# A token's second expert unit reads its partial row, and sums, norms and stores the finished row

## The chip, the cores and the metric

The kernel runs on one core of a Trainium2 chip, as one program. The metric is the device time of one execution in microseconds (us); less is better. The five engines are TensorE (PE), VectorE (DVE), ScalarE (ACT), GpSimd (POOL) and SyncE (SP); each takes its own instructions in order, and they wait for each other through semaphores. DMAs are issued from the queues of SyncE, ScalarE and GpSimd and run on 16 DMA engines.

## What is computed

Two transformer blocks over 512 tokens of width 1024, in float32. The first has sparse and sliding-window attention and a dense MLP; the second has gated linear attention, pooling, and a mixture of experts with a final norm. The change touches only the last of these:

```python
g_p, g_idx = lax.top_k(softmax(ht @ w_rg + b_rg), 1)         # one of 4 groups for each token
e_top, e_idx = lax.top_k(logits_of_that_group, 2)            # two of its 8 experts
gate = g_p * softmax(e_top)
y = (silu(h @ w_gate[e]) * (h @ w_up[e])) @ w_down[e]        # each expert, on its tokens
x = x + sum_of_two(gate * y)
out = x * rsqrt(mean(x * x) + eps) * norm_f_g                # the final norm
```

There are 32 experts (width 256); 512 tokens with two experts each make 1024 rows.

## The kernel before

The first 1040 us compute everything up to the router. The rest is the expert stage and the end. Rows are put into columns of 64: one column for each expert, and one extra column (number 16) for the rows of an expert that has more than 64. Two columns make a unit of 128 rows (unit 8 holds the extra column alone, with 64 rows twice over), so there are 17 units, 0 to 16 (`UNITS_E`, `LAST_E`). Columns of units 0 to 7 hold experts 0 to 15; the later ones hold the late experts, whose numbers are computed. If the expert that overflows is a late one, the extra unit takes it whole, and one column (`SPARE`, 18) has no expert.

For each unit, GpSimd gathers the tokens' rows from `x_rows` in DRAM into one of five buffers `xe` (L682); TensorE transposes them (L1945), and VectorE scales the result into `xeT` (L1687). TensorE multiplies by the gate and up weights `gu` (L2287); ScalarE applies Silu (L1106), VectorE the product (L1694), TensorE transposes, ScalarE copies to `hidT` (L1109), and TensorE multiplies by the down weights `dn` (L2304). VectorE multiplies by the gate and adds into `xe` (L1702, function `y_of`), which signals `y_made`. As each row of x was stored halved, the two rows of a token together hold x once. GpSimd scatters the unit's rows to `y2_rows` in DRAM (L686): the first choice of token t goes to row t, the second to row 512 + t.

SyncE loads the weights; a buffer is loaded again as soon as its unit is done (six buffers of a column for gate and up, eight for down). The spare column is loaded by GpSimd with indirect DMAs (L696), which skip rows whose number is out of bounds.

GpSimd's order in the loop over q = 0 to 15 is written out: at q = 7 the three loads of the spare column; then wait for `y_made` of unit q, scatter it, wait that the scatter of unit q-1 has landed, gather the rows of unit q+4. VectorE's order is: hidden product of unit q, transposed rows of unit q+2, `y_of(q)`.

At the end (L645 to L653) SyncE waits for the scatters of units 0 to 15 and reads both planes of `y2_rows` back, one block of 128 tokens after another. The last unit's rows are not scattered: TensorE puts them into place by a product with a one-hot matrix (`hot`, L2413) and for two blocks adds the planes too (L2419). VectorE sums (L1868, L1875), ScalarE squares (L1135 to L1144), VectorE refines the root (L1164 to L1167) and multiplies (L1877, L1884), SyncE stores `out` (L651).

The lists that all this goes by are made on VectorE between 1040 and 1092 us: `tabi` (rows and slots of each column), `slotv` (their factors), from the rank counts `pos`, `late_columns`, `place_overflow`, `list_overflow` and `name_late_experts`.

Of the kernel before, what the change touches and what calls it, by code (L numbers as in the profile page):

```python
# [5 lines left out]
F32 = mybir.dt.float32  # L6
# [7 lines left out]
P = 128  # L14
# [27 lines left out]
def late_at(n):  # L42


    c = (n - 2 * EXTRA_AT + 1) // 2
    return c - 1 if n % 2 else PAIRS - 1 if n == SPARE else c + PAIRS // 2 - 2


def places_of(q):

    return (2 * q, 2 * q + 1) if q < EXTRA_AT else (2 * q,) if q == EXTRA_AT else (2 * q - 1, 2 * q)
# [26 lines left out]
def expert_at(n):  # L78

    return n if n < 2 * EXTRA_AT else None  # L80
# [155 lines left out]
def gated_blocks(nc, A, out):  # L236
# [8 lines left out]
    with stack:  # L245
# [35 lines left out]
        def const(name, rows=P):  # L281
# [37 lines left out]
                 for n, at in mix_at.items()}  # L319
# [45 lines left out]
        tabi, over_n, steps64, over_at, spare_rows, tab_end = lay(low_at + words([P, 2, NK, P]) + words([P, 2, DE]),  # L365
                                       ("tabi", [P, 2, COLS], I32), ("over_n", [1, 2 * OVER + 1], I32), ("steps64", [P, 8]),
                                       ("over_at", [P, 2], I32), ("spare_rows", [P, 1], I32))
# [7 lines left out]
        y2 = place("y2", [P, NT, 2, D], top + 2 * half_buf)  # L375
        x_out = place("x_out", [P, 2, NT, P], base + 4 * CONST_COLS["cos"][0])
        zeros = place("zeros", [P, D], s_at + 2 * half_buf)
        hot = place("hot", [P, NT, P], base + 4 * CONST_COLS["before"][0])
# [9 lines left out]
        y2_rows = nc.dram_tensor("y2_rows", [2 * L, D], F32).ap()  # L388
# [33 lines left out]
        def for_overflow(e, over, block_of):  # L422
            with e.If(over > 1):
                with e.Fori(1, OVER) as i:
                    block_of(i)
                e.wait_ge(S("over_scattered"), 16 * (OVER - 1))
# [13 lines left out]
        def _(sp):  # L440
# [59 lines left out]
            for q in range(QUARTERS):  # L500
# [16 lines left out]
                for n in range(2 * q, 2 * q + 2):  # L517
                    sp.dma_start(y2_rows[n * P:(n + 1) * P, :], zeros[:, :]).then_inc(S("y_zeroed"), 16)
# [137 lines left out]
        def _(pool):  # L656
# [19 lines left out]
            row_bound, slot_bound = pool.to_reg(L - 1), pool.to_reg(2 * L - 1)  # L676
# [8 lines left out]
            def scatter(n, slots, done):  # L685
                pool.indirect_dma_start(y2_rows, bass.IndirectOffsetOnAxis(ap=slots, axis=0), xe[:, n, :], None,  # L686
                                        bounds_check=slot_bound, oob_is_err=False).then_inc(done, 16)
# [16 lines left out]
            pool.wait_ge(S("y_zeroed"), 16 * 2 * NT)  # L704
# [14 lines left out]
            def overflow(i):  # L719
# [5 lines left out]
                gather((LAST_E - 1) % X_BUFS, over_at[:, 1:2], S("over_gathered"))  # L725
# [4 lines left out]
                scatter((LAST_E - 1) % X_BUFS, over_at[:, 0:1], S("over_scattered"))  # L730

            pool.wait_ge(S("scattered1"), 16 * LAST_E // 2)
            for_overflow(pool, over, overflow)
            for n in range(X_BUFS):
# [14 lines left out]

# [1710 lines left out]
```

## Time and profile before

| what | us |
|---|---|
| median of 3 runs | 1302.31 |
| lowest, highest | 1302.14, 1302.82 |
| the profiled execution | 1302.32 |
| its span, first to last instruction | 1300.0 |
| TensorE busy in the span | 1267.6 (98%) |
| VectorE, ScalarE, GpSimd busy | 613.1, 460.4, 535.5 |
| mean granted TensorE clock | 0.994 of full |

The span is what the trace covers; a little lies around it. Busy time of TensorE counts matmuls in flight, so 98% is not TensorE at its peak. What a change to one stage does has to be read from that stage: its share of DMA, its waits, and the chain that ends last in it.

### The profile page before, as it was taken

How to read it: one execution, taken by the hardware profiler on the slowest of the kernel's cores; microseconds unless marked ns; L12 is line 12 of the kernel's file. 1: busy time of each engine (PE TensorE's matmuls, PEld its weight loads, DVE VectorE, ACT ScalarE, POOL GpSimd, SP SyncE). 2: the span in 40 equal slices, each digit the busy share in tenths (PEclk: the TensorE clock that was granted, in tenths of full speed). 3: DMA queues.
4: the chain of work that ended last, by engine and by line, in shares of the span. 5: the costliest groups of instructions: out<-in, count | busy, mean ns of one | idle time of the engine just before them, and what ended most of it. 6: DMA issues, size and time to landing. Idle time of an engine off the chain costs nothing.

```text
span 1300.0 us, 18634 instructions
## 1 busy us (share of the span) xinstructions
PE 1267.6 (98%) x6670; PEld 968.7 (75%) x6670; DVE 613.1 (47%) x1162; ACT 460.4 (35%) x770; POOL 535.5 (41%) x685
## 2 busy tenths in 40 slices
PE   8999999999999999999999999999999999999986
PEld 6767777787888888888888788777888875555552
DVE  4868768725542422222225765757243265222225
ACT  5657534435434324133144534145322210000102
POOL 4633323334555655555545664424644211121100
PEclk9999999999999999999999999999999999999999
DMA  7422222112334433434333333312426989999995
GB/s 221 107 65 56 66 58 66 50 49 81 98 96 113 131 97 97 130 98 129 97 98 114 97 93 85 83 49 67 128 81 268 362 323 394 424 421 424 424 423 240
DMA packets 212157, 211.38 MB, mean 163 GB/s; under 512 B 31903, under 2 KB 193425, under 8 KB 200817
## 3 DMA queue, kind: packets, MB, share of 16 engines
q1 hardware_dynamic: 203104, 200.25, 45.8%
q0 software_dynamic: 5184, 8.29, 1.7%
q10 hardware_dynamic: 3796, 1.86, 0.5%
q8 instruction: 46, 0.75, 0.2%
q14 instruction: 27, 0.22, 0.0%
HBM read 205.76 MB, written 16.78 MB: 171 GB/s over the span
## 4 chain that ended last, share of the span: by engine, by line
issue 39%; POOL 31%; PE 26%; DMA 1%; DVE 1%; POOLq 0%; ACT 0%; SPq 0%; DVEq 0%; ACTq 0%
POOL wlo L661 31%; PE bank L2287 8%; PE bank L2304 4%; PE bank L1915 3%; PE bank L1917 3%; PE bank L1916 3%; PE side L1945 2%; DMA y<-y_rows 1%; PE bank L1956 1%; DMA y_rows<-xe,tabi 1%; PE side L1917 1%; PE side L1915 1%; PE side L1916 1%; PE side L2203 1%; PE bank L2419 0%
## 5 line engine op out<-in xcount | busy, mean ns | idle before, releaser
L661 POOL TENSOR_TENSOR wlo<-raw,whi 128x256 fp32r<-128x256 f32 x644 | 498.2, 805 | 524.4 <-ACT whi L785 524.2
L1916 PE MATMUL bank<-actB_lo,whi 128*128 128x512 f32 x608 | 236.7, 389 | 0.0
L1915 PE MATMUL bank<-actB_hi,whi 128*128 128x512 f32 x576 | 227.7, 395 | 0.5 <-POOL wlo L661 0.5
L1917 PE MATMUL bank<-actB_hi,wlo 128*128 128x512 f32 x576 | 224.4, 390 | 0.0
L785 ACT ACTIVATE whi<-raw 128x1024 fp32r<-128x1024 f32 x161 | 169.0, 1051 | 151.8 <-PE bank L1917 124.9
L1915 PE MATMUL bank<-actA_hi,whi 128*128 128x512 f32 x400 | 157.3, 393 | 0.6 <-DVE actA_lo L1201 0.6
L1916 PE MATMUL bank<-actA_lo,whi 128*128 128x512 f32 x400 | 156.1, 390 | 0.0
L1917 PE MATMUL bank<-actA_hi,wlo 128*128 128x512 f32 x400 | 156.1, 390 | 0.0
L2287 PE MATMUL bank<-gu,xeT 128*64 128x256 f32 x1088 | 127.7, 384 | 4.7 <-issue 2.2
L1916 PEld LDWEIGHTS bank<-actB_lo,whi 128*128 128x128 f32 x608 | 114.2, 188 | 24.1 <-issue 1.0
L1915 PEld LDWEIGHTS bank<-actB_hi,whi 128*128 128x128 f32 x576 | 108.1, 188 | 25.9 <-issue 2.3
L1917 PEld LDWEIGHTS bank<-actB_hi,wlo 128*128 128x128 f32 x576 | 108.1, 188 | 22.8
L2287 PEld LDWEIGHTS bank<-gu,xeT 128*64 128x64 f32 x1088 | 80.7, 138 | 46.9 <-issue 15.2
L1938 PE MATMUL bank<-actA_hi,whi 128*128 128x512 f32 x216 | 95.0, 440 | 0.0
L1915 PEld LDWEIGHTS bank<-actA_hi,whi 128*128 128x128 f32 x400 | 75.5, 189 | 17.6 <-DVE actA_lo L1201 1.8
L1916 PEld LDWEIGHTS bank<-actA_lo,whi 128*128 128x128 f32 x400 | 75.5, 189 | 15.8 <-issue 0.2
L1917 PEld LDWEIGHTS bank<-actA_hi,wlo 128*128 128x128 f32 x400 | 75.4, 188 | 15.7
L686 POOL DMA_INDIRECT y_rows<-xe,tabi x16 | 16.3, 1018 | 168.4 <-DVE xe L1702 168.4
L1940 PE MATMUL bank<-actA_hi,wlo 128*128 128x512 f32 x216 | 85.0, 394 | 0.0
L1939 PE MATMUL bank<-actA_lo,whi 128*128 128x512 f32 x216 | 84.4, 391 | 0.0
L1396 DVE TENSOR_SCALAR relu_u<-bank 128x512 f32<-128x512 f32 x32 | 22.1, 692 | 128.7 <-PE bank L1917 128.7
L1106 ACT ACTIVATE hid<-bank,slotv 128x256 f32<-128x256 f32 x17 | 12.6, 740 | 167.8 <-PE bank L2287 167.8
(433 smaller groups left out, 1653.0 us busy)
## 6 DMA issues: line engine op xcount, KB each, us to landing
dn<-in_w_exp_down SPq DMA_DIRECT2D x32, 1024.0 KB, 16.0
raw<-in_w_in SPq DMA_DIRECT2D x57, 512.0 KB, 3.8
gu<-in_w_exp_gate SPq DMA_DIRECT2D x28, 1024.0 KB
gu<-in_w_exp_up SPq DMA_DIRECT2D x28, 1024.0 KB
raw<-in_w_up SPq DMA_DIRECT2D x32, 512.0 KB, 3.9
raw<-in_w_down SPq DMA_DIRECT2D x32, 512.0 KB, 3.6
raw<-in_w_out SPq DMA_DIRECT2D x16, 512.0 KB, 3.7
raw<-in_w_in SPq DMA_DIRECT2D x16, 256.0 KB, 3.1
```

Source lines behind the costliest of these rows:

```text
L661: ins = nc.gpsimd.tensor_tensor(wlo[:, slot, at], raw[:, slot, at], whi[:, slot, at].bitcast(F32), ALU.subtract)
L785: a(whi[:, c % RING, :], raw[:, c % RING, :], ACT.Copy).then_inc(hi_made, 1)
L1396: chain(v.tensor_scalar(relu_u[:, m % 2, :], out_bank(up + m)[:, :], 0.0, None, ALU.max), chunk_freed)
L1915: mm(b[:, :], w_hi, hi[:, k, :], start=first, stop=False)
L1916: mm(b[:, :], w_hi, lo[:, k, :], start=False, stop=False)
L1917: ins = mm(b[:, :], w_lo, hi[:, k, :], start=False, stop=last)
L1938: mm(b[:, :], w_hi, actA_hi[:, k, :], start=k == 0, stop=False)
L1939: mm(b[:, :], w_hi, actA_lo[:, k, :], start=False, stop=False)
L1940: ins = mm(b[:, :], w_lo, actA_hi[:, k, :], start=False, stop=k == NK - 1)
L1945: return nc.tensor.transpose(dst, src, ident[0:src.shape[0], 0:src.shape[0]])
L2287: ins = mm(b[ROWS * h:ROWS * (h + 1), g * DE:(g + 1) * DE], xeT[:, j, k, ROWS * h:ROWS * (h + 1)], gu[n % GU_BUFS][:, g, k, :], start=k == ...
L2304: ins = mm(bank[2 + n][ROWS * h:ROWS * (h + 1), :], hidT[:, j, k * P + ROWS * h:k * P + ROWS * (h + 1)], w[:, k, n * L:(n + 1) * L], start ...
```

## The change

No plane of y is read back at the end. The stored x is no longer halved. Each row has a turn: the earlier of a token's two units scatters x + its part to `part_rows` (512 rows instead of 1024); the later unit does not gather its x into the sum, but gathers the partial row over its `xe` row after TensorE has transposed it, adds its own part, and so has the finished row, which is squared (ScalarE, `squares_of`), normed (VectorE, `finish`) and stored straight to `out` by an indirect DMA (`store_rows`). Rows that a list leaves out carry a number out of bounds and are skipped. This holds for units 2 to 16. So that a token's two experts are never in neighbouring units, experts are renumbered: column n of the first 16 holds expert 8 (n mod 4) + n // 4.

GpSimd's order for each unit becomes: store of unit q-1, scatter of unit q, wait for that scatter's landing, gather of the partial rows of unit q+1, wait for the store's landing, gather of the x rows of unit q+4. VectorE gets `finish(q-1)`, which waits for the scatter of q-1, ahead of `y_of(q)`, and `y_of(q)` waits for its partial rows. ScalarE gets two table loads for each unit. At the end TensorE's one-hot products and sums, VectorE's sums and SyncE's reads and stores are gone; unit 16 goes the same way as the others.

The diff, cut to what matters (the overflow loop, which takes no part here, is left out):

```diff
 def expert_at(n):
-    return n if n < 2 * EXTRA_AT else None
+    return EPG * (n % NG) + n // NG if n < 2 * EXTRA_AT else None
+OVER_X = (LAST_E + 1) % X_BUFS
+FINISH_FROM = 2
...
         @block.sync
-            for j in range(2):
-                sp.wait_ge(S(f"scattered{j}"), 16 * LAST_E // 2)
-            for i in range(NT):
-                sp.dma_start(y2[:, i, :, :], y2_rows.rearrange("(k t p) n -> t p k n", k=2, p=P)[i])\
-                  .then_inc(S(f"block_in{i}"), 16)
-            for i in range(NT):
-                sp.wait_ge(S("final_out"), i + 1)
-                sp.dma_start(out[i * P:(i + 1) * P, :], y2[:, i, 1, :]).then_inc(S("stored"), 16)
-            sp.wait_ge(S("stored"), 16 * NT)
+            sp.wait_ge(S("rows_stored"), 16 * (UNITS_E - FINISH_FROM))
...
         @block.gpsimd
+            def gather_parts(n, tokens, done):
+                pool.indirect_dma_start(xe[:, n, :], None, part_rows, bass.IndirectOffsetOnAxis(ap=tokens, axis=0),
+                                        bounds_check=row_bound, oob_is_err=False).then_inc(done, 16)
+
+            def store_rows(n, tokens, done):
+                pool.indirect_dma_start(out, bass.IndirectOffsetOnAxis(ap=tokens, axis=0), xe[:, n, :], None,
+                                        bounds_check=row_bound, oob_is_err=False).then_inc(done, 16)
+
+            def scattered(q):
+                pool.wait_ge(S(f"scattered{q % 2}"), 16 * (q // 2 + 1))
+
+            def parts_of_unit(q):
+                pool.wait_ge(S("xe_used"), 2 * (q + 1))
+                gather_parts(q % X_BUFS, tabi[:, 2, q:q + 1], S("parts_in"))
+
+            def store_unit(q):
+                pool.wait_ge(S("rows_finished"), q - FINISH_FROM + 1)
+                store_rows(q % X_BUFS, tabi[:, 2, q:q + 1], S("rows_stored"))
...
             for q in range(LAST_E):
                 if q == EXTRA_AT - 1:
+                    pool.wait_ge(S("slots_ready"), 2)
                     spare_expert()
+                if q > FINISH_FROM:
+                    store_unit(q - 1)
                 pool.wait_ge(S("y_made"), q + 1)
                 scatter(q % X_BUFS, tabi[:, 0, q:q + 1], S(f"scattered{q % 2}"))
+                if FINISH_FROM <= q + 1 < LAST_E:
+                    scattered(q)
+                    parts_of_unit(q + 1)
                 n = q - 1 + X_BUFS
                 if n < UNITS_E:
                     if q == 0:
                         pool.wait_ge(S("over_listed"), 1)
                     else:
-                        pool.wait_ge(S(f"scattered{(q - 1) % 2}"), 16 * ((q - 1) // 2 + 1))
+                        scattered(q - 1)
+                    if q > FINISH_FROM:
+                        pool.wait_ge(S("rows_stored"), 16 * (q - FINISH_FROM))
                     gather(n % X_BUFS, tabi[:, 1, n:n + 1], S(f"gathered{n % X_BUFS}"))
...
+            parts_of_unit(LAST_E)
+            store_unit(LAST_E - 1)
+            store_unit(LAST_E)
+            pool.wait_ge(S("rows_stored"), 16 * (UNITS_E - FINISH_FROM))
...
         @block.scalar
+            def squares_of(q):
+                one_ = slice(q % NT, q % NT + 1)
+                nc.scalar.preload_act_table_set("natural_log_exp_and_others")
+                for n in range(2):
+                    act.wait_ge(*((S("y_made"), q + 1) if q < LAST_E else (S("last_y_made"), n + 1)))
+                    chain(a(side[3][:, :], xe[:, q % X_BUFS, n * L:(n + 1) * L], ACT.Square, accum_out=gw[:, 10 + n, one_]))
+                    if n == 0:
+                        chain(a(gw[:, 3, one_], gw[:, 10, one_], ACT.Identity, scale=1.0 / D, bias=eps_t[:, :]))
+                chain(a(gw[:, 14, one_], gw[:, 11, one_], ACT.Ln, scale=1.0 / D, bias=gw[:, 3, one_]))
+                chain(a(gw[:, 13, one_], gw[:, 14, one_], ACT.Exp, scale=-0.5), S("guess_made"))
             for q in range(LAST_E):
...
+                if q >= FINISH_FROM:
+                    squares_of(q)
+                    if q < LAST_E - 1:
+                        nc.scalar.preload_act_table_set("silu_and_others")
...
         @block.vector
             def y_of(q):
                 dve.wait_ge(S("down_done"), q + 1)
+                if q >= FINISH_FROM:
+                    dve.wait_ge(S("parts_in"), 16 * (q - FINISH_FROM + 1))
...
+            def finish(q):
+                one_ = slice(q % NT, q % NT + 1)
+                dve.wait_ge(S("guess_made"), guesses[0] + 1)
+                chain(v.tensor_tensor(gw[:, 12, one_], gw[:, 10, one_], gw[:, 11, one_], ALU.add))
+                refine(gw[:, 12, one_], gw[:, 13, one_], D, gw[:, 14, one_], gw[:, 15, one_])
+                if q < LAST_E:
+                    dve.wait_ge(S(f"scattered{q % 2}"), 16 * (q // 2 + 1))
+                chain(v.scalar_tensor_tensor(xe[:, q % X_BUFS, :], xe[:, q % X_BUFS, :], gw[:, 13, one_], gfin[:, :],
+                                             ALU.mult, ALU.mult), S("rows_finished"))
...
+                if q == 1:
+                    list_overflow()
                 if q + 2 < UNITS_E:
                     rows_turned(q % 2, q + 3)
-                if q == 1:
-                    list_overflow()
+                if q > FINISH_FROM:
+                    finish(q - 1)
                 y_of(q)
```

The lists get some more small VectorE steps: whose turn it is (`vals[:, :, 0]`), the tokens to finish (`tokens_to_finish`), the renumbering in `late_columns` and `name_late_experts`.

## Rows read from the trace of the kernel before

**Rows 1.** Windows: length, busy of PE, PEld, DVE, ACT, POOL, clock, DMA share, GB/s.

```profile
1112.00:1124.00 12.00, 12.00 (x92) 6.66 (x90) 3.12 (x6) 1.13 (x2) 2.03 (x2) 1.00 1.01 422
1252.00:1269.50 17.50, 14.55 (x100) 7.88 (x96) 2.08 (x4) 1.41 (x3) 1.84 (x2) 0.90 0.98 411
1269.50:1275.00 5.50, 4.08 (x34) 2.39 (x35) 0.66 (x1) 0.98 (x3) 0.00 (x0) 1.00 0.37 148
```

**Rows 2.** Chain that ended last, 1225 to 1300 us: start, duration, what.

```profile
1250.18 1.42 DVE xe L1702 x2
...
1251.87 0.99 POOL y_rows L686
...
1267.41 7.44 DMA y_rows<-xe,tabi
...
1275.89 10.13 DMA y<-y_rows
...
1296.20 0.75 DVE y L1884
```

**Rows 3.** VectorE timeline, 1053 to 1270 us: start, duration, what, idle before.

```profile
1079.47 0.69 DVE L1694 SCALAR_TENSOR_TENSOR hid<-bank,slotv,hid 128x256 f32<-128x256 f32 x1
...
1086.52 1.41 DVE L1702 SCALAR_TENSOR_TENSOR xe<-bank,slotv,xe 128x512 f32<-128x512 f32 x2 [3.32 <-PE bank L2304]
...
1098.54 1.41 DVE L1702 SCALAR_TENSOR_TENSOR xe<-bank,slotv,xe 128x512 f32<-128x512 f32 x2 [4.26 <-PE bank L2304]
...
1265.72 1.41 DVE L1702 SCALAR_TENSOR_TENSOR xe<-bank,slotv,xe 128x512 f32<-128x512 f32 x2 [6.56 <-PE bank L2304]
```

**Rows 4.** Page: span, software DMA queue (packets, MB, share of engines).

```profile
span 1300.0 us, 18634 instructions
...
q0 software_dynamic: 5184, 8.29, 1.7%
```

**Rows 5.** Line 686, scatter of a unit: ns, and us to landing.

```profile
DMA to landing us min/median/max: 7.4/8.1/9.7
```

**Rows 6.** Timeline of all engines, 1048 to 1058 us.

```profile
1049.64 1.20 POOL L682 DMA_INDIRECT xe<-x_rows,tabi  x1 [3.39 <-DVE tabi L1639]
...
1050.09 1.28 ACT L1094 ACT_TABLE_LOAD   x1
...
1051.04 0.17 DVE L1656 COPY vals<-con 128x8 f32<-128x8 f32 x1
...
1054.93 0.95 PEld L1945 LDWEIGHTS side<-con,xe 128*128 128x128 f32 x8 [0.31 <-DMA xe<-x_rows,tabi]
```

**Rows 7.** Line 682, gather of a unit, 1040 to 1060 us.

```profile
L682 POOL DMA_INDIRECT xe<-x_rows,tabi x4: 992/996/1196, 1049.6 to 1053.7; - x4
...
DMA to landing us min/median/max: 4.4/4.4/4.4
```

**Rows 8.** Line 682, 1080 to 1300 us.

```profile
DMA to landing us min/median/max: 10.0/10.0/10.1
```

**Rows 9.** DMAs issued 1112 to 1113.5 us (unit 3): count, landing.

```profile
y_rows<-xe,tabi POOLq DMA_INDIRECT x1, 8.5
```

**Rows 10.** Timeline of all engines, 1255 to 1300 us.

```profile
1269.46 3.67 PE L2287 MATMUL bank<-gu,xeT 128*64 128x256 f32 x32 [0.33 <-DMA gu<-in_w_exp_up]
...
1278.71 0.75 DVE L1854 SCALAR_TENSOR_TENSOR xe<-bank,slotv,xe 128x512 f32<-128x512 f32 x1 [0.97 <-PE bank L2404]
...
1291.85 0.60 ACT L1139 ACTIVATE xe<-bank 128x512 f32<-128x512 f32 x1
...
1292.91 1.28 DVE L1877 SCALAR_TENSOR_TENSOR y<-y,gw,gfin 128x1024 f32<-128x1024 f32 x1
...
1294.01 0.29 ACT L1143 ACTIVATE gw<-gw 128x1 f32<-128x1 f32 x1
```

**Rows 11.** DMA issues, 1040 to 1300 us.

```profile
out<-y SPq DMA_DIRECT2D x4, 512.0 KB, 2.6
...
gu<-in_w_exp_gate,spare_rows POOLq DMA_INDIRECT x1
```

More of the change, by code:

```diff
@@ L516, in _ @@
                 load_group(C_MLP + 2 * NK * q + NK, NK, w_down_v[:, NK * q:NK * (q + 1), :], 0)
-                for n in range(2 * q, 2 * q + 2):
-                    sp.dma_start(y2_rows[n * P:(n + 1) * P, :], zeros[:, :]).then_inc(S("y_zeroed"), 16)
+                sp.dma_start(part_rows[q * P:(q + 1) * P, :], zeros[:, :]).then_inc(S("y_zeroed"), 16)
             for j, n, col in IN2_GROUPS:
@@ L1613, in _ @@
             chain(v.tensor_scalar(two, rest, 1.5, None, ALU.is_lt))
-            chain(v.tensor_tensor(picks_r[:, 0:NT, :].rearrange("p t (g e) -> p t g e", g=NG), of_group, by_group(two), ALU.mult),
+            chain(v.tensor_tensor(picks_r[:, 0:NT, :].rearrange("p t (e g) -> p t g e", g=NG), of_group, by_group(two), ALU.mult),
                   S("picks_made"))
@@ L1637, in _ @@
             chain(v.tensor_tensor(shifted, lg[:, :, 0:NG], spread(gw[:, 0, :], NG), ALU.subtract), S("shifted"))
+            apart = gw[:, 9, :]
+            chain(v.tensor_scalar(pos_q[:, :], pos[:, :], ROWS - 0.5, None, ALU.is_lt))
+            chain(v.tensor_tensor(rest, two, one, ALU.subtract))
             dve.wait_ge(S("table_full"), 1)
             chain(v.tensor_scalar(tabi[:, 1, 0:EXTRA_AT], bank[1][:, 0:EXTRA_AT], float(SKIP), None, ALU.add), S("rows_ready"))
+            chain(v.tensor_tensor(rest, rest, const("iota")[:, 0:EPG].unsqueeze(1).broadcast_to([P, NT, EPG]), ALU.mult))
+            chain(v.tensor_reduce(apart, rest, AX, ALU.add))
             for n, pick in ((4, one), (5, two)):
@@ L1643, in _ @@
             chain(v.tensor_tensor(gw[:, 6, :], gw[:, 5, :], gw[:, 4, :], ALU.subtract), S("shifted"))
-            second_rows = placed[:, NT:2 * NT, 0, 0:LATE]
-            chain(v.scalar_tensor_tensor(second_rows, picks8[:, NT:2 * NT, 0:LATE], float(L), second_rows, ALU.mult, ALU.add))
+            firsts, seconds = slice(0, NT), slice(NT, 2 * NT)
+            for mine, other, after in ((firsts, seconds, ALU.is_lt), (seconds, firsts, ALU.is_gt)):
+                chain(v.scalar_tensor_tensor(vals[:, mine, 0], apart, 0.0, pos_q[:, other], after, ALU.mult))
+            chain(v.scalar_tensor_tensor(vals[:, :, 0], vals[:, :, 0], float(L), row_at[:, :], ALU.mult, ALU.add))
+            chain(v.tensor_tensor(placed[:, :, 0, 0:LATE], picks8[:, :, 0:LATE], every(vals[:, :, 0], LATE), ALU.mult))
             dve.wait_ge(S("exps_made"), 1)
@@ L1655, in _ @@
             by_k = vals[:, :, :].rearrange("p (k t) n -> p k t n", k=2)
[L1656 removed]
             for k in range(2):
[L1658 removed]
+                chain(v.tensor_copy(by_k[:, k, :, 1], norm))
             chain(v.tensor_tensor(by_k[:, 0, :, 2], gw[:, 2, :], gw[:, 8, :], ALU.mult))
@@ L1763, in place_overflow @@
                                       vals[:, :, 1:3].unsqueeze(3).broadcast_to([P, 2 * NT, 2, EVENS + ODDS]), ALU.mult))
+                turn, last = first_at, at_odd
+                chain(v.tensor_scalar(turn, pos[:, :], EVENS - 0.5, -float(EVENS), ALU.is_ge, ALU.mult))
+                chain(v.tensor_tensor(turn, turn, pos[:, :], ALU.add))
+                chain(v.tensor_scalar(last, turn, float(LAST_E - EXTRA_AT), 1000.0, ALU.is_equal, ALU.mult))
+                chain(v.tensor_tensor(turn, turn, last, ALU.add))
+                for mine, other in ((firsts, seconds), (seconds, firsts)):
+                    chain(v.tensor_tensor(vals[:, mine, 0], turn[:, mine], turn[:, other], ALU.is_gt))
+                chain(v.scalar_tensor_tensor(vals[:, :, 0], vals[:, :, 0], float(L), row_at[:, :], ALU.mult, ALU.add))
                 chain(v.tensor_tensor(in_col, in_col, every(vals[:, :, 0], EVENS + ODDS), ALU.mult), S("over_placed"))
@@ L1850, in _ @@
             hidden(LAST_E % 2, slotv[:, 0, LAST_E:LAST_E + 1], UNITS_E, bank[1 - LAST_E % 2][:, DE:])
+            finish(LAST_E - 1)
+            dve.wait_ge(S("parts_in"), 16 * (UNITS_E - FINISH_FROM))
             for n in range(2):
```

184 lines of the change are left out of this document (88 added, 96 removed).

## The prediction

> **What bounds the kernel now.** I read the windows by stage first: from 1087 us to 1269.5 us, while the experts run, the DMA engines are full (share 1.01, 422 GB/s), and from 1269.5 us they fall to 0.37 [rows 1]. So the stretch with the expert weights is set by what the DMA engines deliver, and a tail follows. Then the chain that ended last, in order of time: scatter of unit 15 (7.44 us), read of the y plane (10.13 us), sums and norm, last product at 1296.20 us [rows 2]. Then the timeline of VectorE: the add that makes a unit's rows ("y add", two instructions, 1.41 us) starts at 1086.52 us for unit 1, at 1098.54 us for unit 2 and at 1265.72 us for unit 15 [rows 3]; that is (1265.72 - 1098.54) / 13 = 12.86 us per unit. I call the end of a unit's y add its T: T1 = 1087.93, T15 = 1267.13. The tail behind T15 is 1300.0 - 1267.13 = 32.9 us [rows 2, 4].
>
> In the kernel before, no unit waits for another unit's scatter: it lands while the next unit runs. That is what the change gives up. Sums are made against the profiled span of 1300.0 us [rows 4]; this execution took 1302.32 us, so 2.3 us lie around the span, and the median of the runs is 1302.31. A measurement here tells a change of over 0.2% (2.6 us) from none.
>
> **A new chain through the DMA queue.** In the new order of GpSimd, after the scatter of unit q comes a wait for its landing, then the gather of the partial rows of unit q+1, and the y add of unit q+1 waits for that gather. VectorE's y add of q+1 releases the next scatter. So one unit costs at least: y add end to scatter issue 0.27 us (1250.18 + 1.42 to 1251.87) [rows 2]; landing of the scatter, 7.4 to 9.7 us, median 8.1 [rows 5]; about 0.3 us to the next issue (an estimate from the same 0.27); landing of the gather; y add 1.41 [rows 3]. For a gather that has its queue to itself beside full weight traffic the nearest row is the first one: issued at 1049.64, TensorE's first transpose released by it at 1054.93, 5.3 us [rows 6]. The shortest landing is 4.4 us, when the weights had run out [rows 7]; one issued 1.3 us behind a scatter takes 10.0 [rows 8]. The partial gather is issued when the scatter has landed, so I take 5.3: 0.27 + 8.1 + 0.3 + 5.3 + 1.41 = **15.4 us**, against 12.86 now. Fewer real rows in each (512 first rows are scattered, 512 gathered) should not help: the landings differ by at most 2.3 us over units that, by the router's counts, hold 32 to 94 rows, and the one with 32 (unit 3) took 8.5 [rows 9].
>
> GpSimd's queue also carries four indirect DMAs for each unit instead of two: finished rows out, scatter, partial gather, x gather. Today's pair tells what a second one costs: scatter 8.1 after its issue, the gather behind it 1.3 + 10.0 = 11.3 after that, so 3.2 us more [rows 5, 8]. If all hold the queue for 3.2, the x gather and the store ahead of the next scatter are gone in time and nothing is added (15.4). If a write holds it for 8.1 - 5.3 + 3.2 = 6.0 us, the next scatter waits behind the store, and with the same sum in the steady state the unit comes to about 21 us. At that cadence the weights no longer fill the DMA engines (6.3 MB of weights and 0.66 MB of rows per 21 us), which relieves it. I take **17.0 us**, nearer to the low end, with 15.4 and 19 for the range.
>
> What the Trainium skill states on such a DMA ("DMA: Bandwidth & Descriptors", Anatomy of one DMA, SWDGE path) is 2.0 us and bytes over 436 GB/s; for 64 rows of 4 KB an estimate from that page is 2.6 us, and by it the chain of a unit would be near 7 us and hidden. The trace has 7.4 to 9.7 us for a scatter [rows 5] and does not agree; rival (a) is what it would bring.
>
> The cover ends with the weights. Weight buffers hold three units ahead, so with units 13 to 15 the queue of weights is empty and landings shorten. With 7.4 and 4.4 [rows 5, 7] a unit costs 13.8; I take 13 for the last two periods, with 12 and 16 as ends.
>
> **A second loop, shorter.** ScalarE now squares unit q's rows between two units: two halves of 0.60 + 0.2, three small steps of 0.3, 0.3 and 0.2, and a table load of 1.28 back to Silu [rows 6, 10]; the other table load is done before the rows are there. From T: 2.5 + 1.3, Silu and product 1.4, transpose and copy 1.1, down 3.6, y add 1.4, in all 11.3 us (durations of the tail's rows [rows 10] and their like in each unit). That is under 15.4, so it costs nothing as long as the DMA chain is the longer. VectorE's finish of unit q-1 (five small steps of 0.16 and one of 1.28 [rows 10]) waits for the scatter's landing ahead of the y add; it lies beside the partial gather: nothing. Behind it on VectorE queue only that y add and, behind this, the next hidden product, which the 11.3 holds.
>
> **The spare expert.** The change renumbers experts as 4 times the place in the group plus the group. By the reference's router on these inputs one expert has more than 64 rows: 89, first of group 2, number 16 before and 2 after. Today it counts as a late one, which leaves one column without an expert, and its indirect loads (issued from GpSimd [rows 11]) skip all rows but one: 1024 gathered and 992 scattered rows of 4 KB and three of 8 KB are 8.28 MB, and the software queue moved 8.29 [rows 4]. With number 2 no late expert is free, so the spare loads 128 x 24 KB = 3.15 MB: 7.5 us at 422 GB/s [rows 1], in the queue ahead of the store of unit 6 and the scatter of unit 7. At half the rate, as it shares with the weights, it takes 15 us and the scatter of unit 7 comes up to 12 late; I take 8, with 0 to 12.
>
> **Ahead of the chain.** Router values: net 4 more small VectorE steps of 0.2 before they are placed, 0.8 us; placing the overflow: net 7 more, 1.4 us, on the path, since VectorE goes into the hidden product of unit 1 with no idle time [rows 3]. The steps added to the late columns fit into idle time before unit 0's y add. Listing the overflow ahead of a transposed block delays only a unit needed later. Small steps are 0.17 us each [rows 6]. Half as many zeroed rows long before: nothing.
>
> **The sum.** T1 = 1087.9 + 2.3 = 1090.2. T2 = + 15.4 = 1105.6. T3 to T13: 11 x 17.0 = 187. T14, T15: 26. Spare: 8. T15 = 1326.6. Tail: 0.27 + scatter of 15 landing 7.4 + 0.5 + partial gather 4.4 to 5.3 + two halves 1.5 + last squares and root 1.4 + finish 2.3 + 0.3 + store of the last rows landing 4.4 to 7.4 (a plain store takes 2.6 [rows 11]) + about 0.5 at the end, together 23 to 26, taken 25 (before: 32.9). Unit 16's own matmuls are shorter than the 13 us of scatter and gather. 1351.6 + 2.3 = **1354 us**. So the read of the y plane and its sums (1275.89 to 1296 [rows 2]) do go, and give back 8 us; the chain takes 59. Low end: 11 x 15.4 + 24, no cost for the spare, tail 23: 1324. High end: 11 x 19 + 32, spare 12, tail 26: 1387.
>
> **Rivals.**
> (a) The landings of today are long only by what shares the queue with them, the new ones are near the 2.6 us of a plain store of 512 KB on quiet engines [rows 11], the chain is hidden, and weight traffic alone binds. Then the last weights land at 1269.5 + 7.5 (spare) + 4.7 (some 480 more rows of 4 KB moved until then, 2.0 MB at 422) = 1281.7; from there to the end of unit 16's y add 10.0 us (1269.46 to 1279.46 [rows 10]), then 1.4 + 2.3 + 0.3 + 4.4 to 7.4 + 0.5: 1300.6 to 1303.6, so 1303 to 1306 us. Against it: every scatter's landing in the trace, that of unit 15 too, which lands at 7.4 while the engines fall to 0.37 [rows 1, 2]. The page above speaks for it. 6%.
> (b) The chain binds, but with landings of 7.4 and 4.4: 13.8 x 14 from 1090.2 is 1283.4, and with 3 for the spare, tail 23 and 2.3: about 1312 us. For it: writes of half as many rows. Against it: the weights keep the engines full until unit 12. 9%.
> (c) The software queue itself is the bound, 21 us a unit throughout: 1105.6 + 11 x 21 + 32 + 12 + 26 + 2.3 = 1409 us. 7%.
> (d) The other side: the chain is hidden and the spare expert costs nothing, so that only the tail counts: (a) less 7.5, 1295 to 1298 us. It decides if scatter and gather together land within 11.2 us (14 steps from 1090.2, with the tail of 25, must end by 1300.0: 13.2 a unit, less the 2.0 of issue and y add), where the trace's shortest two make 11.8. 3%.
> (e) The gathers bring so little that nothing measurable moves: 1%.
>
> **Chances.** Forecast (1324 to 1390) 74%, the rest as above. The range leaves out (a), (d), (e), (c) and the short end of (b): 1320 to 1390. Faster by over 0.2%: 3%. Within: (e) and half of (a), 4%. Slower: 93%.
>
> **What would show it.** In the profile after: y adds of VectorE 15 to 19 us apart from unit 2 on, waiting for the gather from the partial rows; TensorE idle a fifth to a third of the time between 1100 and 1320 us; DMA share under 1 there, lowest in the last three units; 13.6 MB in the software queue (2560 rows of 4 KB and 3.15 MB); no read of the y plane; a tail of 23 to 26 us behind unit 15's y add. If the y adds are 12 to 13 us apart, the chain argument is wrong, and (a) or (d) holds.

## The result, and the profile after

| | before | after |
|---|---|---|
| median, us | 1302.57 | 1371.71 |
| lowest, highest of 4 runs | 1302.14, 1303.10 | 1366.50, 1376.38 |
| ratio, 95% interval | | 1.053, 1.0484 to 1.0575 |
| profiled span, us | 1300.0 | 1374.6 |
| mean granted TensorE clock | 0.994 | 0.967 |
| software DMA queue, MB | 8.29 | 13.66 |

The change makes the kernel 5.3% slower: 69 us, where 52 were forecast. The runs of the changed kernel are 10 us apart, those of the kernel before 1. The profiled execution is the longest of the four (1376.38), so the trace holds some 4.7 us more than the median.

The y adds of the changed kernel first, as in [rows 3]: VectorE's timeline (start, duration, what, idle time before it and what ended it).

```profile
1077.88 1.41 DVE L1750 SCALAR_TENSOR_TENSOR xe<-bank,slotv,xe 128x512 f32<-128x512 f32 x2 [0.80 <-PE bank L2376]
1093.72 1.41 DVE L1750 SCALAR_TENSOR_TENSOR xe<-bank,slotv,xe 128x512 f32<-128x512 f32 x2 [2.34 <-PE bank L2376]
1113.09 1.41 DVE L1750 SCALAR_TENSOR_TENSOR xe<-bank,slotv,xe 128x512 f32<-128x512 f32 x2 [11.54 <-DMA xe<-part_rows,tabi]
1131.30 1.41 DVE L1750 SCALAR_TENSOR_TENSOR xe<-bank,slotv,xe 128x512 f32<-128x512 f32 x2 [7.17 <-DMA xe<-part_rows,tabi]
...
1195.61 1.41 DVE L1750 SCALAR_TENSOR_TENSOR xe<-bank,slotv,xe 128x512 f32<-128x512 f32 x2 [3.46 <-PE bank L2376]
1225.23 1.41 DVE L1750 SCALAR_TENSOR_TENSOR xe<-bank,slotv,xe 128x512 f32<-128x512 f32 x2 [6.33 <-DMA xe<-part_rows,tabi]
...
1322.58 1.41 DVE L1750 SCALAR_TENSOR_TENSOR xe<-bank,slotv,xe 128x512 f32<-128x512 f32 x2 [8.67 <-DMA xe<-part_rows,tabi]
1335.85 1.41 DVE L1750 SCALAR_TENSOR_TENSOR xe<-bank,slotv,xe 128x512 f32<-128x512 f32 x2 [3.49 <-PE bank L2376]
1349.40 1.41 DVE L1750 SCALAR_TENSOR_TENSOR xe<-bank,slotv,xe 128x512 f32<-128x512 f32 x2 [3.19 <-PE bank L2376]
```

In [rows 3] the down product (PE) released every one of them. Now the partial gather does for ten of fourteen. Steps from unit 1 to unit 15: 19.4, 18.2, 16.7, 20.1, 14.2, 13.3, 29.6, 19.0, 21.0, 17.1, 19.1, 21.2, 13.3, 13.6 us. What GpSimd does between two of them (its timeline, units 2 and 3):

```profile
1114.78 1.02 POOL L676 DMA_INDIRECT part_rows<-xe,tabi  x1 [7.55 <-DVE xe L1750]
1123.01 2.01 POOL L680 DMA_INDIRECT xe<-part_rows,tabi  x1 [7.21 <-DMA part_rows<-xe,tabi]
1125.33 0.99 POOL L672 DMA_INDIRECT xe<-x_rows,tabi  x1 [0.31 <-issue]
1126.62 1.02 POOL L684 DMA_INDIRECT out<-xe,tabi  x1 [0.30 <-issue]
...
1132.99 0.99 POOL L676 DMA_INDIRECT part_rows<-xe,tabi  x1 [5.34 <-DVE xe L1750]
```

These are the scatter of unit 2, 8.2 us until it has landed and the gather of unit 3's partial rows is issued, and then 8.3 us until the y add at 1131.30. The waits from 1100 to 1375 us (engine and line, waited for what: us in total, times, longest) say the same of all units:

```profile
POOL xe L680 <- DMA part_rows<-xe,tabi: 104.6, 15, 19.5
DVE xe L1750 <- DMA xe<-part_rows,tabi: 77.1, 10, 11.5
DVE xe L1761 <- DMA part_rows<-xe,tabi: 29.1, 10, 13.5
PE side L2017 <- DMA xe<-x_rows,tabi: 23.5, 8, 5.3
```

Last the windows by stage (stretch, length, busy us and count of PE, PEld, DVE, ACT, POOL, then granted clock, DMA share, GB/s), to be held against [rows 1]:

```profile
1100.00:1320.00 220.00, 166.53 (x1058) 88.31 (x1059) 58.94 (x126) 66.46 (x123) 59.55 (x49) 0.85 0.89 354
...
1169.00:1184.00 15.00, 11.05 (x61) 5.09 (x61) 5.65 (x12) 6.15 (x12) 5.07 (x5) 0.77 0.52 184
...
1324.00:1337.00 13.00, 8.34 (x40) 4.10 (x42) 4.90 (x11) 5.88 (x11) 3.03 (x3) 0.74 0.12 38
```

TensorE is busy 166.5 of 220 us, so idle a quarter of the time. The DMA engines are no longer full. In each of these stretches, in all of which TensorE was idle for a part, the granted clock is below full (0.85, 0.77, 0.74).

### The profile page after: what moved, and what is told of

Read it like the earlier page. It is cut to its first block, busy times and chain, and to the rows that moved or that the text cites. A ratio compares the mean times of both kernels' runs of the same rounds, so it can differ in the third digit from the quotient of the medians.

```text
span 1374.6 us, 18853 instructions
## 1 busy us (share of the span) xinstructions
PE 1277.9 (93%) x6642; PEld 969.4 (71%) x6642; DVE 632.4 (46%) x1240; ACT 522.2 (38%) x884; POOL 575.9 (42%) x715
## 3 DMA queue, kind: packets, MB, share of 16 engines
q0 software_dynamic: 9504, 13.66, 2.9%
## 4 chain that ended last, share of the span: by engine, by line
issue 46%; POOL 33%; PE 14%; DMA 4%; DVE 1%; ACT 1%; POOLq 0%; DVEq 0%; ACTq 0%; SPq 0%
POOL wlo L651 29%; PE bank L1987 3%; PE bank L1989 3%; PE bank L1988 3%; PE bank L2359 2%; POOL xe L680 1%; DMA part_rows<-xe,tabi 1%; PE bank L2376 1%; DMA xe<-x_rows,tabi 1%; DMA xe<-part_rows,tabi 1%; PE side L2017 1%; POOL out L684 1%; POOL xe L672 1%; POOL part_rows L676 1%; PE side L1989 1%
## 5 line engine op out<-in xcount | busy, mean ns | idle before, releaser
L2359 PE MATMUL bank<-gu,xeT 128*64 128x256 f32 x1088 | 137.3, 406 | 16.5 <-issue 10.9
L2376 PE MATMUL bank<-dn,hidT 128*64 128x512 f32 x256 | 69.1, 689 | 2.8 <-ACT hidT L1136 2.8
L1144 ACT ACTIVATE side<-xe 128x512 f32<-128x512 f32 x30 | 18.0, 601 | 136.5 <-DVE xe L1750 133.6
## 6 DMA issues: line engine op xcount, KB each, us to landing
dn<-in_w_exp_down SPq DMA_DIRECT2D x32, 1024.0 KB, 12.5
```

The source lines that it names most:

```text
L1144: chain(a(side[3][:, :], xe[:, q % X_BUFS, n * L:(n + 1) * L], ACT.Square, accum_out=gw[:, 10 + n, one_]))
L2359: ins = mm(b[ROWS * h:ROWS * (h + 1), g * DE:(g + 1) * DE], xeT[:, j, k, ROWS * h:ROWS * (h + 1)], gu[n % GU_BUFS][:, g, k, :], start=k == ...
L2376: ins = mm(bank[2 + n][ROWS * h:ROWS * (h + 1), :], hidT[:, j, k * P + ROWS * h:k * P + ROWS * (h + 1)], w[:, k, n * L:(n + 1) * L], start ...
```

## The experiments

Medians are of four runs each, the ratio is to the kernel before on the same chip. The changed kernel is the 1371.7 us above, timed on its own, and its runs lie 10 us apart, so differences to it of about 5 us are within the spread; where a kernel is said to save no more than that, the trace carries the argument. Below, T1 and T15 are the ends of the y adds of units 1 and 15, as in the prediction. Each kernel differs from the changed kernel unless it says otherwise.

**Is it the chain?** Partial rows gathered from `x_rows`, which are there at once, and GpSimd doesn't wait for its scatter:

```diff
-                pool.indirect_dma_start(xe[:, n, :], None, part_rows, ...
+                pool.indirect_dma_start(xe[:, n, :], None, x_rows, ...
...
-                    scattered(q)
                     parts_of_unit(q + 1)
```

> Two edits on the changed kernel, one thing undone: the gather of partial rows reads from the x rows, which nothing writes in this stage, and GpSimd does not wait for the landing of the unit's own scatter before it (the sums are wrong; number, size and skipped rows of the gathers are the same). Theory (the wait from scatter to gather is what costs): the y adds are 13 to 14.5 us apart, bound by ScalarE's and TensorE's loop, except at the spare; the time falls by 35 to 50 us, to 1322 to 1337. Rival (four DMAs for each unit fill the software queue, whatever waits for what): the y adds stay 17 us or more apart while the weights are loading, and the time stays over 1355.

Measured: 1319.6 us (1.0128, 1.0099 to 1.0157), 52 us less, with the same bytes and the same four DMAs a unit. The windows show full DMA engines again:

```profile
1100.00:1170.00 70.00, 66.13 (x484) 36.06 (x486) 27.50 (x60) 31.15 (x57) 20.64 (x21) 1.00 1.02 421
```

Steps are 12.1 to 13.8 us except for the one at the spare expert (26.6) and the last (14.8). So waiting for two landings in a row in each unit costs 52 of the 69 us. The other 17 lie, by the spans, as follows: 7.2 us up to T1, 10.7 in the step at the spare expert (26.6 against 15.9 in the kernel before), some 8 in the other thirteen steps (13.2 against 12.6 each), less 9.1 in the tail. In this kernel the DMA engines are full until 1289 us, as they were until 1269.5 in the kernel before, which speaks for their traffic setting the time again.

**Do the stores crowd the queue?** The finished rows of units 2 to 14 are not stored:

```diff
-                if q > FINISH_FROM:
-                    store_unit(q - 1)
...
-                        pool.wait_ge(S("rows_stored"), 16 * (q - FINISH_FROM))
+                        pool.wait_ge(S("rows_finished"), q - FINISH_FROM)
```

> One thing left out of the changed kernel: the finished rows of units 2 to 14 are not stored (so out lacks them), which takes one of the four DMAs for each unit out of the software queue; the chain from scatter to gather is as it was. Theory (the part of the step that exceeds the forecast comes from the scatter waiting behind a store and an x gather in its queue): the median landing of the scatter falls under 7.5 us, and each step by 1 to 2 us, in all 12 to 25 us less. Rival (the landings are as long as they are because of the weights in the other queue): landings and time as in the changed kernel, less than 5 us apart.

Measured: 1366.4 us (1.0477, 1.0452 to 1.0503). The landing of the scatters (us, shortest, median, longest) is as in the changed kernel, whose median is 8.0:

```profile
DMA to landing us min/median/max: 2.1/7.9/18.4
```

So one indirect DMA less in each unit did not shorten the landings. The 5.3 us between the medians are at the edge of the spread, and fall far short of the 12 to 25 expected; in the traces (in both cases the longest of four runs) T1 to T15 is 9.6 us shorter. By these traces the stores cost some 0.7 us a unit, not the 1.6 that the prediction put on crowding, and the rival stands in the main.

**VectorE's wait for the final gains.** In the changed kernel VectorE waits for all small inputs, the final norm's gains among them, before it turns unit 0's rows. The wait is moved to unit 3's first norm:

```diff
-            dve.wait_ge(S("small_in"), 16 * (N_SMALL + 1))
             rows_turned(0, 1)
...
+                if q == FINISH_FROM + 1:
+                    dve.wait_ge(S("small_in"), 16 * (N_SMALL + 1))
                 if q > FINISH_FROM:
                     finish(q - 1)
```

> One edit on the changed kernel: VectorE's wait for the load of the final norm's gains stands ahead of unit 3 again, not ahead of unit 0's transposed rows. The trace after the change shows VectorE idle 6.5 us there, and TensorE's first gate product 4.3 us later than before. Theory (the wait is 4.3 us on the path, and the DMA chain passes a start that is earlier on to the end): 4 to 5 us less than the changed kernel, about 1367. Rival (the weights are late at the start as well, so nothing is gained): the same as the changed kernel within its own spread of 5 us, with unit 1's y add ending as late as now.

Measured: 1365.2 us (1.0474, 1.0456 to 1.0492), with the y adds of units 0 and 1 3.5 us earlier. The median is 6.5 us lower, of which only these 3.5 can be seen in the trace. VectorE's first scaling of rows, in the changed kernel and then in this one:

```profile
1060.04 1.29 DVE L1733 TENSOR_TENSOR xeT<-side,small 128x512 f32<-128x512 f32 x2 [6.50 <-DMA gfin<-in_norm_f_g]
```

```profile
1058.12 1.29 DVE L1733 TENSOR_TENSOR xeT<-side,small 128x512 f32<-128x512 f32 x2 [2.62 <-PE side L2018]
```

**The spare expert.** Its loads are put out of bounds (expert 31 computes with old weights):

```diff
-                chain(v.tensor_tensor(at_end, at_end, late, ALU.mult))
```

> One edit on the changed kernel: the spare column's row numbers are set out of bounds as they were before the change, so that its 3.15 MB are not loaded (expert 31's rows get a wrong part). Theory (the spare stands ahead of unit 7's scatter in the software queue): the landing of that scatter falls from 20.2 us to 8 to 10, the step from unit 7's to unit 8's y add from 29.6 us to 17 to 19, and the time by 10 to 12 us, to about 1361. Rival (it costs only its share of the DMA traffic, 7.5 us at most, and the engines are not full there): under 4 us less.

Measured: 1363.1 us (1.0485, 1.044 to 1.053), with runs 18 us apart (1352.2 to 1370.0). Then the same with the right output: experts numbered with the upper half of each group first, so that the overflowing expert is number 18, a late one, and the spare column stays without an expert as in the kernel before:

```diff
-    return EPG * (n % NG) + n // NG if n < 2 * EXTRA_AT else None
+    return EPG * (n % NG) + (n // NG ^ EPG // 2) if n < 2 * EXTRA_AT else None
```

> The changed kernel with another numbering of the experts, results the same: the upper four of each group come first, so that the expert with 89 rows is number 18, a late one, and the spare column is skipped as before the change (four more small VectorE steps ahead, about 0.8 us). Theory (the numbering cost what leaving out the spare's loads gained, 8.6 us between the medians): 6 to 12 us less than the changed kernel, software queue 10.5 MB, no step over 23 us. Rival (what the spare cost is then paid at another unit, since other units hold the rows): less than 4 us gained.

Measured: 1359.3 us (1.0423, 1.0378 to 1.0468); the longest step falls from 29.6 to 23.7 us and the longest scatter landing from 20.2 to 13.9. Between medians the spare costs 9 to 12 us, and with runs 12 and 18 us apart this is no more than a rough figure. Only part of the long step is its bytes. Where they are left out it still takes 22.4 and 23.7 us (15.9 in the kernel before; 17 to 19 and at most 23 were expected), and the scatter of unit 7 still takes 14.5 and 13.9 us to land behind three loads that skip nearly every row. Those loads keep their packets, since the count of the queue is the same with and without the bytes (changed kernel first, then this one):

```profile
q0 software_dynamic: 9504, 13.66, 2.9%
```

```profile
q0 software_dynamic: 9504, 10.54, 2.3%
```

**Does VectorE's norm hold GpSimd up?** The norm's product is one column wide for units 2 to 14:

```diff
-                chain(v.scalar_tensor_tensor(xe[:, q % X_BUFS, :], xe[:, q % X_BUFS, :], gw[:, 13, one_], gfin[:, :],
+                chain(v.scalar_tensor_tensor(xe[:, q % X_BUFS, 0:n_], xe[:, q % X_BUFS, 0:n_], gw[:, 13, one_], gfin[:, 0:n_],
```

> One edit on the changed kernel: the product that norms a finished row is one column wide for units 2 to 14 instead of 1024 (those rows of out are then not normed), so VectorE no longer works from SBUF to SBUF for 1.28 us just when GpSimd issues the gather of partial rows. Theory (this product holds up the GpSimd instruction, which takes 2.0 us there against 1.0 elsewhere): the median of the gather's instruction falls to 1.0 us, steps fall by about 1 us each, 8 to 12 us less in all. Rival (the 2.0 us are the gather's own, from the tensor it reads): still 2.0 us, and the time within 5 us of the changed kernel.

Measured: 1367.4 us (1.0508, 1.0485 to 1.0531). GpSimd's gather instruction (ns, shortest, median, longest), changed kernel first:

```profile
L680 POOL DMA_INDIRECT xe<-part_rows,tabi x15: 1016/2022/2027, 1104.9 to 1354.1; - x15
```

```profile
L680 POOL DMA_INDIRECT xe<-part_rows,tabi x15: 1016/1035/1042, 1105.0 to 1341.6; - x15
```

It is shown that the product lengthens the instruction by 1.0 us. The 8 to 12 us expected of this in time did not come: the median is 4 us lower, within the spread. The Trainium skill ("SBUF — State Buffer", SBUF: two separate sides) has a VectorE instruction with two SBUF inputs and a GpSimd instruction that reads SBUF exclude each other on a shared port pair; the trace agrees in kind, with 1.0 us for a product of 1.28.

**Can the chain be hidden?** The partial rows of unit q+1 come from units up to q-1 only (but for units 7 and 8, which the renumbering leaves neighbours for some token), so their gather need not wait for the scatter of q. It is issued ahead of it, once the scatter of q-1 has landed:

```diff
+                if FINISH_FROM <= q + 1 < LAST_E and q + 1 != EXTRA_AT:
+                    if q:
+                        scattered(q - 1)
+                    parts_of_unit(q + 1)
                 if q > FINISH_FROM:
                     store_unit(q - 1)
                 pool.wait_ge(S("y_made"), q + 1)
...
-                if FINISH_FROM <= q + 1 < LAST_E:
+                if q + 1 == EXTRA_AT:
                     scattered(q)
```

> The changed kernel with one order changed: the partial rows of unit q+1 are gathered once the scatter of unit q-1 has landed, ahead of the scatter of unit q, since on these inputs no token's two units are neighbours but units 7 and 8 (there the wait stays as it was). All DMAs, bytes and results are those of the changed kernel. Theory (the landing of the unit's own scatter on the chain is what costs): steps of 12.5 to 14 us but at units 8 and 9, and 35 to 50 us less than the changed kernel, 1320 to 1335. Rival (real dependences through DRAM keep the landing on the chain whatever the distance, or the queue is full): steps stay over 16 us and the time over 1350.

Measured: 1335.7 us (1.0253, 1.023 to 1.0275), 36 less. The steps are 11.8 to 16.6 us (31.1 at the spare), where 12.5 to 14 were expected. The wait of the y add for the gather is gone but at one unit, and the first and third of these waits grew (waits from 1100 to 1320 us; L1765 is the norm of unit q-1, which stands ahead of the y add of q on VectorE):

```profile
POOL xe L672 <- DMA out<-xe,tabi: 60.9, 8, 9.2
POOL xe L680 <- DMA part_rows<-xe,tabi: 60.5, 13, 20.5
DVE xe L1765 <- DMA part_rows<-xe,tabi: 59.2, 10, 16.5
```

The norm works in place, on the buffer that the scatter is still reading, so it waits for the landing. Then all that had helped together: this order, the late wait, the numbering by halves, and ScalarE squaring unit q-1 behind the next unit's Silu instead of unit q ahead of it:

```diff
-                if q >= FINISH_FROM:
-                    squares_of(q)
+                if q > FINISH_FROM:
+                    squares_of(q - 1)
```

> The changed kernel with four edits together, results the same: partial rows gathered two units back (waits as in the change only at units 8 and 11), ScalarE squares a unit's rows behind the next unit's Silu and copy instead of ahead of them, the wait for the final gains ahead of unit 3, and the numbering that skips the spare. Theory (chain, second loop, moved wait and spare are all that the change lost, and the end then shows its gain): the weights bind again, 12 to 13.3 us a unit but for steps of 16 to 19 us at units 8 and 11, a tail of 22 to 24 us, and 1293 to 1305, from 9 us less than the kernel before to the same. Rival (four indirect DMAs a unit and the scatter ahead of the norm keep it at 13.5 us or more): 1312 or more.

Measured: 1320.1 us (1.0137, 1.012 to 1.0154), with steps of 14.6 us on average, so the rival held. Its span is 18.6 us over that before: 2.8 up to unit 1's y add, 24.8 from there to unit 15's (204.0 against 179.2), and 9.0 given back by the tail. The late wait and the numbering alone had given 6.5 and 12.4 us, together more than the 15.6 that lie between the last two kernels; the order on ScalarE was not run by itself, and no gain of its own shows. A part of the 24.8 is that the weights are in later. The DMA engines are full but for one stretch (windows), and fall only from 1281 to 1285 us, where they had fallen at 1269.5:

```profile
1100.00:1280.00 180.00, 155.13 (x1092) 86.07 (x1090) 63.17 (x133) 70.91 (x132) 54.26 (x49) 0.94 0.99 406
...
1180.00:1210.00 30.00, 26.94 (x188) 14.71 (x188) 9.69 (x21) 11.86 (x22) 9.99 (x9) 0.89 0.86 335
```

That is some 12 to 15 us, with the 2.8 up to T1 among them. On top of it y adds come late after the down product, that of unit 12 for example (timeline):

```profile
1246.98 1.03 POOL L672 DMA_INDIRECT xe<-x_rows,tabi  x1 [7.40 <-DMA out<-xe,tabi]
...
1249.57 1.28 DVE L1772 SCALAR_TENSOR_TENSOR xe<-xe,gw,gfin 128x1024 f32<-128x1024 f32 x1 [2.92 <-DMA part_rows<-xe,tabi]
1249.74 2.00 POOL L680 DMA_INDIRECT xe<-part_rows,tabi  x1 [1.73 <-DMA part_rows<-xe,tabi]
1250.89 1.41 DVE L1761 SCALAR_TENSOR_TENSOR xe<-bank,slotv,xe 128x512 f32<-128x512 f32 x2
```

The y add follows the norm with no idle time, the norm waited for the scatter. It did so in six units, 14.2 us in total. In five others ScalarE's squares, which now come later, held the norm until about the end of the down product, and the y add began 1.6 to 2.1 us behind that. TensorE waited 16.3 us for x rows. How much each of these is worth in time was not separated. To take the norm off that path, the kernel was run once more with the y add ahead of it, and the scatter ahead of the store:

```diff
-                if q > FINISH_FROM:
-                    finish(q - 1)
                 y_of(q)
+                if q > FINISH_FROM:
+                    finish(q - 1)
```

> The kernel of the experiment before (1320.1 us) with one change of order: VectorE adds unit q's rows first and norms unit q-1 behind it, so that the wait for the landing of the scatter of q-1 (about 9.5 us) stands behind the y add and no longer ahead of it; GpSimd scatters q first and stores q-1 after it. Theory (the in-place norm puts each scatter's landing back on the path from y add to y add): steps between y adds fall from 14.6 us on average to 12.5 to 13.3, the rate of the weights, and the time falls by 15 to 25 us, to 1295 to 1305. Rival (the x rows of unit q+4 are gathered only when the store of q-1 has landed, in one of five buffers; that gather now comes some 3 us later and takes the norm's place as what is waited for): TensorE's waits for the x rows grow from 16 us to 30 or more, and the time stays within 5 us of 1320.

Measured: 1340.2 us (1.0294, 1.0277 to 1.0311), 20 slower. Seven of fourteen steps are now 12.0 to 13.3 us, as the theory has it, but four are 20.8, 26.2, 21.0 and 20.9. TensorE's wait for x rows, in the kernel of the experiment before (from 1100 to 1300 us) and in this one (1100 to 1320):

```profile
PE side L2033 <- DMA xe<-x_rows,tabi: 16.3, 6, 3.9
```

```profile
PE side L2033 <- DMA xe<-x_rows,tabi: 31.2, 8, 8.6
```

This is one of the long steps (timeline):

```profile
1230.45 1.04 POOL L672 DMA_INDIRECT xe<-x_rows,tabi  x1 [9.88 <-DMA out<-xe,tabi]
1231.81 1.01 POOL L676 DMA_INDIRECT part_rows<-xe,tabi  x1 [0.31 <-issue]
...
1238.80 1.97 PE L2033 MATMUL side<-con,xe 128*128 128x128 f32 x8 [5.40 <-DMA xe<-x_rows,tabi]
...
1241.53 1.03 POOL L680 DMA_INDIRECT xe<-part_rows,tabi  x1 [8.72 <-DMA part_rows<-xe,tabi]
...
1249.32 1.41 DVE L1761 SCALAR_TENSOR_TENSOR xe<-bank,slotv,xe 128x512 f32<-128x512 f32 x2 [7.82 <-DMA xe<-part_rows,tabi]
```

GpSimd waits 9.9 us for a store to land, because the x rows of a later unit go into its buffer. The scatter, whose rows were ready at 1229.7, stands behind that wait, the partial gather behind the scatter. The rival's wait came as it said (31.2 us), but its time, within 5 us of 1320, did not: not only the x rows are late, all behind them on the queue are. One in-order queue has to wait for two landings a unit, and each of the three orders tried leaves one of them ahead of something that is due.

**The end.** From the issue of the last store to the end of the span it is 8.5 us (9.0 in the kernel with all parts), where a plain store from SyncE took 3.0 (1296.98 to 1300.0). GpSimd's own final waits are taken out of that kernel; SyncE alone waits:

```diff
-            pool.wait_ge(S("rows_stored"), 16 * (UNITS_E - FINISH_FROM))
-            for n in range(X_BUFS):
-                pool.wait_ge(S(f"gathered{n}"), 16 * ((LAST_E - n) // X_BUFS + 1))
```

> The kernel of the experiment before (1320.1 us) without GpSimd's own final waits for the stores and gathers; SyncE alone waits for the last store. The last store is issued 8.5 to 9 us before the span ends, and its packets are through 2.5 us after the issue. If it is GpSimd's wait that costs the rest, the end comes 3 to 6 us earlier (1314 to 1317). If it is the landing itself or the end of GpSimd's queue, nothing changes (1319 to 1321).

Measured: 1323.0 us (1.0149, 1.0128 to 1.017), against 1.012 to 1.0154: no gain where 3 to 6 us were looked for. The stretch from issue to end was 6.7 us in its trace, 2.3 less, but that store was issued 5.7 us later (1315.33 against 1309.65), which this edit does not explain. Whether GpSimd's wait costs the 2.3 us, and what fills the rest of the end, is open.

No kernel tried beats the one before.

## Why the prediction was right or wrong

The sign, the mechanism and the range held; the time was 17.7 us too low. Against the profiled spans (1374.6 against 1351.6 forecast, 23.0 more), step by step:

| term | forecast | after | off by |
|---|---|---|---|
| T1 | 1090.2 | 1095.1 | +4.9 |
| T2 | 15.4 | 19.4 | +4.0 |
| T3 to T13, without the spare's surcharge | 187 | 198 | +11 |
| the spare's surcharge | 8 | 11.6 | +3.6 |
| T14, T15 | 26 | 26.8 | +0.8 |
| tail | 25 | 23.8 | -1.2 |

(Of the eleven steps the ten without the spare average 18.0, and that of the spare is 29.6, 11.6 over this. The last column adds up to the 23.0 but for rounding.)

**T1** is a step that was missing. The sum counted VectorE's new instructions ahead of unit 0 and not a wait that the diff moved there. The gains' DMA is issued at 1053.66; VectorE stands 6.50 us until it is there, ahead of a step that does not use them. Of the 4.9 us the late wait gave back 3.5; the rest was not traced.

**The chain of a unit** had the right links, and one of them was sized wrong. Scatter landing: taken 8.1 from [rows 5], median 8.0 after. Landing of the partial gather: taken 5.3 from [rows 6], the first gather of the stage, which was not alone in its queue either (three more followed 1.3 us apart [rows 7]); the ten that a y add waited for took 8.4 on average (5.4 to 10.2, from the start of the gather to that of the y add). The other row at hand was 10.0 [rows 8], which the prediction read as queueing behind a scatter; in the changed kernel the gather has its scatter landed before it and still takes nearly that. The surcharge of 1.6 us for crowding, on top of it, had the wrong reason: without the stores the gathers took 8.6 on average and the time fell by 5 us, about the spread. The term that was mis-sized is the gather, by 3.1 us a unit, of which the surcharge happened to cover half. That the average step of 18.0 is so near the 17.0 taken is partly luck: the nine steps other than the spare's in which the chain was what ended last took 19.1 us on average (scatter and issue 8.9, gather 8.5, and 1.7), and the steps of units 6 and 7, 14.2 and 13.3, which waited for the down product, brought the average down. Up to one of the 3.1 may be the instruction itself, 2.02 instead of 1.02 us (with the narrow norm ten gathers took 8.0 on average, and one beside quieter engines 3.8); that the norm beside it is not free was not foreseen (VectorE's finish was put at nothing). The rest is open: the DMA engines were full at the first gather as well (share 0.97 from 1049 to 1055 us), so full engines alone do not tell the two apart, and the gather of x rows that follows 1.3 us behind each partial gather was not taken away.

**T14 and T15** came out as forecast by luck, since it was by another route. With the weights gone a scatter lands in 2.1 to 2.3 us, not 7.4, so the DMA chain no longer binds, and the second loop does. That had been put at 11.3 us and is 13.3 (chain that ended last):

```profile
1322.58 1.42 DVE xe L1750 x2
1324.02 0.73 ACT side L1144 x2
...
1326.41 1.28 ACT L1159
1327.70 0.71 ACT hid L1133
...
1330.51 5.24 PE bank L2376 x16
1335.76 6.92 PE bank L2359 x64
```

The path is y add, squares, table load, Silu, product, transpose, and the down product, which takes 5.24 us at a granted clock of 0.74 where the sum had 3.6. TensorE had been idle ahead of it, and that the idle time which the chain makes lowers the clock is the reading of the windows above, not an experiment. At the last unit the down product is 3.65 again, but the gate and up products of the next unit (6.92) are on the path, and the step is 13.6.

**The spare** was put at 8, and the step is 11.6 us over the others, in its range; the scatter behind its 3.15 MB took 20.2 us to land, and TensorE was idle for 10.9 us ahead of unit 8's gate products, which by the order of the program wait for their weights. But without the bytes 5.5 and 4.0 us of that idle time were still there, and the step was still 6 to 7 us over those kernels' others (22.4 and 23.7 against 16.2 and 16.8): the sum had nothing for loads that skip their rows and yet stand ahead of a scatter that is now waited for. Taking the bytes away gave 9 to 12 in all.

**The tail** held, 23.8 for 25. So did the 13.66 MB, TensorE idle a quarter of the time and the DMA share under 1 (0.89). Of the signs, the y adds 15 to 19 us apart did not: the spare aside they were 13.3 to 21.2.

**The rivals.** (b), the chain binding with short landings (1312): the scatters of units 6 and 13 to 15 landed in 2.1 to 2.5 us, where the DMA engines were quiet (share 0.52 in the window around 1180 us, 0.12 at the end), and there the chain did not bind: the y adds of units 6, 7, 14 and 15 waited for the down product. (c), the queue as the bound at 21 us a unit: two steps reach it, the average is 18, and dropping one of its four DMAs gave 5 us. (a), the hidden chain, 1303 to 1306: even without the chain the time is 1319.6, since the step at the spare is 10.7 us longer than in the kernel before, unit 1's y add 7.2 later, and the DMA engines stay full until 1289 us and not 1281.7.

## What to carry to other kernels

When a change puts a DMA's landing between two units of a pipeline, the cost is the landing as measured beside full traffic, taken over many instances and not from a single first one; here that was 8.4 against 5.3 us, in ten of fourteen units. A dependency of two units' distance instead of one took back half of the loss, but on one in-order queue each wait for a landing holds up everything issued after it, and work in place on a buffer that a DMA reads has to wait for that DMA's landing. Look in a diff for waits that were moved as well as for instructions that were added.

## What had not been expected of the hardware

- A scatter of the same shape lands in 7 to 9.7 us while the DMA engines are full, and in 2.1 to 2.5 while their share is 0.03 to 0.12 (changed kernel, 1184 us and from 1324 us on). The Trainium skill's rule for such a DMA ("DMA: Bandwidth & Descriptors", Anatomy of one DMA, SWDGE path), an estimate of 2.6 us for 64 rows, is near what the quiet engines show and far from what the full ones do. The prediction had left it to rival (a); it had no row of a scatter beside quiet engines.
- A product of VectorE with both inputs in SBUF (128x1024, 1.28 us) lengthens GpSimd's gather instruction beside it from 1.03 to 2.02 us.
- Rows that an indirect DMA skips still have packets: the software queue moved 144 packets for each indirect DMA in every kernel (9504 for 66, 7632 for 53, 5184 for 36), and a scatter behind three loads that skipped nearly all rows took 14 us to land.
- The last indirect store has its packets through 2.5 us after its issue (DMA share 0.36 and 0.12 in the second and third us, none after), but the span goes on for 6 us.
- The runs of the changed kernel and those of the variants of it that keep the chain lie 6 to 18 us apart; those of the kernel before, whose DMA engines are full, 1 to 3.2, and those of the variants without it or with the gather two units back 1 to 8.
